# Output projections of a two-layer decoder step by seven products per pair of chunks, with ring slots as scratch

## What is computed

```python
def short_conv_mixer(x, buf, w_in, conv_w, w_out):
    ...
    y = jnp.einsum('bsc,cd->bsd', gb * conv, w_out)
def rglru_mixer(...):
    ...
    y = jnp.einsum('bsc,cd->bsd', jax.nn.gelu(gate, approximate=True) * h, w_out)
def reference(...):
    for i in range(DEPTH):
        yp, nbp = short_conv_mixer(...)
        xp = layer_norm(ALPHA * xp + yp, ln1_g[i], ln1_b[i])
        mp = hier_moe(xp, ...)
        xp = layer_norm(ALPHA * xp + mp, ln2_g[i], ln2_b[i])
```

## Time and profile before

| | us |
|---|---|
| median of 3 runs | 1436.39 (1434.8 to 1436.47) |
| the profiled execution, its own time | 1436.33 |
| its span, first to last instruction | 1434.6 |
| PE busy | 1364.6 (95%) |
| DVE / ACT / POOL busy | 478.9 / 222.3 / 137.5 |
| read from HBM | 468.77 MB |

### The profile page before, as it was taken

The page is one execution under the profiler, slowest core; times in us unless marked ns, Lnnn a source line. Parts: engine busy times, 40 slices in busy tenths (PEclk is TensorE's granted clock), DMA queues, the critical chain, the costliest instruction groups (busy, mean ns, idle before and its releaser), DMA issues.

```text
span 1434.6 us, 20217 instructions
## 1 busy us (share of the span) xinstructions
PE 1364.6 (95%) x8784; PEld 917.3 (64%) x8784; DVE 478.9 (33%) x1016; ACT 222.3 (15%) x372; POOL 137.5 (10%) x143
## 2 busy tenths in 40 slices
PE   7999999899999999999899999989999999999996
PEld 6888876565555555666468887756655555566661
DVE  5666513412111112132255665163111111113316
ACT  1000002100000000100054554030000000110012
POOL 0000000100010001121000000011100110012201
PEclk9999999999999999999999999999999999999999
DMA  9950273899999999999997113279999999999995
GB/s 263 302 231 0 90 322 108 324 426 425 424 425 423 423 426 423 422 427 422 378 324 322 59 60 120 71 279 417 421 426 425 422 426 424 423 425 424 421 403 209
DMA packets 98543, 472.88 MB, mean 330 GB/s; under 512 B 16607, under 2 KB 51423, under 8 KB 63629
## 3 DMA queue, kind: packets, MB, share of 16 engines
q1 hardware_dynamic: 82509, 449.74, 77.6%
q0 software_dynamic: 11520, 15.52, 3.1%
q10 hardware_dynamic: 4424, 6.30, 1.6%
HBM read 468.77 MB, written 27.32 MB: 346 GB/s over the span
## 4 chain that ended last, share of the span: by engine, by line
PE 66%; DMA 7%; DVE 3%; issue 3%; ACT 3%; POOL 0%; POOLq 0%; DVEq 0%
PE ps L970 26%; PE ps L1006 14%; PE ps L650 8%; PE ps L937 6%; DMA ring<-in_moe_w_down 6%; PE ps L750 3%; PE ps L926 3%; PE ps L948 1%; PE ps L768 1%; DMA yrows<-A,Bt 1%; PE ps L994 1%; ACT A L1316 1%; PE ps L986 1%; DMA ring<-yrows 1%; DVE C L1862 1%
## 5 line engine op out<-in xcount | busy, mean ns | idle before, releaser
L970 PE MATMUL ps<-ring,A 128*64 128x256 f32 x4096 | 455.4, 379 | 7.0 <-ACT A L1292 2.4
L970 PEld LDWEIGHTS ps<-ring,A 128*64 128x64 f32 x4096 | 327.5, 137 | 144.8 <-issue 35.1
L1006 PE MATMUL ps<-ring,A 128*64 128x512 f32 x1024 | 233.8, 597 | 24.9 <-issue 22.0
L1781 DVE TENSOR_TENSOR A<-A,ps 128x256 f32<-128x256 f32 x64 | 27.0, 421 | 558.4 <-ACT A L1304 558.4
L1006 PEld LDWEIGHTS ps<-ring,A 128*64 128x64 f32 x1024 | 76.1, 136 | 137.1 <-issue 130.3
L650 PE MATMUL ps<-A,ring 128*128 128x260 f32 x576 | 130.5, 388 | 2.5 <-DMA ring<-in_a_w_in 2.5
L650 PEld LDWEIGHTS ps<-A,ring 128*128 128x128 f32 x576 | 111.0, 193 | 20.2 <-issue 2.7
L750 PE MATMUL ps<-Bt,ring 128*128 128x260 f32 x512 | 116.1, 385 | 1.0 <-ACT C L1210 0.8
L750 PEld LDWEIGHTS ps<-Bt,ring 128*128 128x128 f32 x512 | 96.1, 190 | 20.1 <-DVE A L1588 2.5
L591 POOL DMA_INDIRECT A<-x,idx x42 | 43.6, 1038 | 656.5 <-PE ps L926 605.6
L937 PE MATMUL ps<-C,Bt 104*64 104x512 f32 x400 | 95.5, 619 | 0.0
(11 more groups left out here) (270 smaller groups left out, 1106.4 us busy)
## 6 DMA issues: line engine op xcount, KB each, us to landing
ring<-in_moe_w_gate SPq DMA_DIRECT2D x62, 2048.0 KB, 20.6
ring<-in_moe_w_up SPq DMA_DIRECT2D x60, 2048.0 KB, 22.4
ring<-in_moe_w_down SPq DMA_DIRECT2D x60, 2048.0 KB, 23.5
ring<-in_a_w_in SPq DMA_DIRECT2D x24, 512.0 KB, 7.2
ring<-yrows SPq DMA_DIRECT2D x10, 1024.0 KB, 9.3
ring<-in_moe_w_up SPq DMA_DIRECT2D x8, 1024.0 KB, 21.7
ring<-in_moe_w_down SPq DMA_DIRECT2D x8, 1024.0 KB, 21.4
ring<-in_b_w_in SPq DMA_DIRECT2D x8, 1024.0 KB, 12.6
```

Source lines behind the costliest of these rows:

```text
L970: mm = pe.matmul(ps[hf * ROWS:(hf + 1) * ROWS, 3, u * FH:(u + 1) * FH], xgT[:, k, :], ring[:, slot, col:col + FH], start=(k == 0), stop=(k ...
L1006: mm = pe.matmul(ps[nh * ROWS:(nh + 1) * ROWS, 2, :], hidT[:, at:at + ROWS], ring[:, slot, m * D + nh * 512:m * D + (nh + 1) * 512], start ...
L1781: tt(gated, gated, ps[:, 3, FH:2 * FH], ALU.mult).then_inc(ready, 1)
```

## The change

Each pair of output chunks (2q, 2q+1) is computed by seven products of 4 matmuls (`out_product`), for the blocks a11, a12 (chunk 2q, features 0 to 511 and 512 to 1023) and a21, a22 (chunk 2q+1). POOL forms the sums S1 to S4 of the weights (`out_sums`: 4 + 12 operations on 128x512 in each layer), DVE the pieces T1 to T4 of `hT` (`out_pieces`, on 128x260). The eight products that need only the first four chunks of `hT` (`EARLY`) come first and are copied to SBUF by ACT; the other twenty (`LATE`) are taken out of PSUM by DVE with adds on 128x260. Products rotate over six PSUM banks, each waiting for its bank to be empty (`bank_free`).

Pieces, sums and copies lie in three ring slots of input weights (`SCRATCH`: slots 0, 1, 2 in layer 0, slots 6, 7, 8 in layer 1), which no expert unit may enter until the projection is over. The first ten expert units are therefore spread over the slots in another order (`CYCLE`), and SP waits for them by `room_count`. In layer 0, five units wait for the first early product, the sixth for product (2, 6), and four for `logits(7)`. In layer 1, one unit goes with each of the input units 0 to 3 and the gate unit, the sixth with product (2, 6), and four with `logits(7)`. The early load of two units at L711 is gone, and so is that of three units in layer 1. Three semaphores of the recurrence become one (`act_gate`), with the same waits.

```diff
+DENSE = U_IN[0] + U_OUT
+CYCLE = ((3, 4, 5, 6, 7, 8, 0, 1, 2, 9), (0, 1, 2, 9, 3, 4, 6, 7, 5, 8))
+SCRATCH = ((0, 1, 2), (6, 7, 8))
 def ring_slot(pos):
-    return pos % RING
...
+    if pos < DENSE:
+        return pos
+    l = int(pos >= POS_EXP[1])
+    return CYCLE[l][(pos - POS_EXP[l]) % RING]
...
+EARLY = [(q, i) for q in range(KT // 2) for i in (1, 5)]
+LATE = [(q, i) for q in range(KT // 2) for i in (6, 7, 4, 3, 2)]
+NPART = len(EARLY) + len(LATE)
+OUT_BANKS = ((5, 3, 0, 1, 2, 4), (0, 1, 2, 3, 4, 5))
+COMPLETE = (1, 0, 3, 2, 5, 4, 7, 6)
...
+def room_count(pos):
+    for l in range(DEPTH):
+        if POS_EXP[l] <= pos < POS_EXP[l] + RING:
+            i = pos - POS_EXP[l]
+            if l == 0:
+                return 5 if i < 5 else 6 if i == 5 else DENSE
+            return freed_after(POS_IN[1] + min(i, U_IN[1] + 1))
+    return freed_after(pos - RING)
...
-                    sp.wait_ge(freed, freed_after(pos - RING))
+                    sp.wait_ge(freed, room_count(pos))
...
+            def out_sums(l):
+                pool.wait_ge(mm_in[l], (PLAIN + 14, 1)[l])
+                for q in range(KT // 2):
+                    if q % 2 == 0:
+                        pos = POS_OUT[l] + q // 2
+                        pool.wait_ge(loaded[ring_slot(pos)], load_target(pos))
+                    a21, a22 = out_part_w(l, 2 * q + 1, 0), out_part_w(l, 2 * q + 1, 1)
+                    pool.tensor_tensor(a21, a21, a22, ALU.add).then_inc(sum_ok, 1)
+                for q in range(KT // 2):
+                    pool.wait_ge(sum_ok, KT * l + (KT // 2 if q == 0 else KT // 2 + q))
+                    if q >= 2:
+                        pool.wait_ge(out_mm, NPART * l + len(EARLY) + 5 * (q - 2) + 4)
+                    a11, a12 = out_part_w(l, 2 * q, 0), out_part_w(l, 2 * q, 1)
+                    s1, a22 = out_part_w(l, 2 * q + 1, 0), out_part_w(l, 2 * q + 1, 1)
+                    s2, s3, s4 = (out_sum(l, q, n_) for n_ in range(3))
+                    step(pool.tensor_tensor(s2, s1, a11, ALU.subtract))
+                    pool.tensor_tensor(s3, a22, s2, ALU.subtract)
+                    pool.tensor_tensor(s4, a12, s2, ALU.subtract).then_inc(sum_ok, 1)
...
-                    if u == 2 and i == 0 and k == 0:
-                        mm.then_inc(freed, 2)
...
+            def out_factors(l, q, i):
+                a11, a12 = out_part_w(l, 2 * q, 0), out_part_w(l, 2 * q, 1)
+                s1, a22 = out_part_w(l, 2 * q + 1, 0), out_part_w(l, 2 * q + 1, 1)
+                w = {1: a11, 2: a12, 3: out_sum(l, q, 2), 4: a22, 5: s1, 6: out_sum(l, q, 0), 7: out_sum(l, q, 1)}[i]
+                x = {1: hT[:, :KH, :HALF], 2: hT[:, KH:, :HALF], 3: hT[:, KH:, HALF:]}
+                t = {5: 0, 6: 1, 7: 2, 4: 3}
+                return w, (lambda k: x[i][:, k, :]) if i in x else (lambda k: out_piece(l, t[i], k))
...
-                def logits(m, free=0):
-                    pe.wait_ge(zT_done, KT * l + m + 1)
-                    if m == 0:
+                def logits(n, free=0):
+                    m = COMPLETE[n]
+                    pe.wait_ge(zT_done, KT * l + n + 1)
+                    if n == 0:
                         pe.wait_ge(wg_ok, l + 1)
                     for hf in range(2):
                         mm = pe.matmul(ps[:NC + 2, 6 + hf, :HALF], wr[:, m, :], xT[:, m, hf * HALF:(hf + 1) * HALF],
-                                       start=(m == 0), stop=False)
+                                       start=(n == 0), stop=False)
                         if free and hf == 0:
                             mm.then_inc(freed, free)
...
+                def early_part(n):
+                    q, i = EARLY[n]
+                    if n in (0, 4):
+                        pos = POS_OUT[l] + n // 4
+                        pe.wait_ge(loaded[ring_slot(pos)], load_target(pos))
+                    bank_free(n)
+                    if i == 5:
+                        pe.wait_ge(piece_ok, 5 * l + 1)
+                        pe.wait_ge(sum_ok, KT * l + q + 1)
+                    out_product(l, q, i, n, free=(5 if (l, n) == (0, 0) else 1 if (l, n) == (1, 4) else 0)
+                                ).then_inc(out_mm, 1)
+                pe.wait_ge(h_done[l], KH)
+                for n in range(4):
+                    early_part(n)
                 if l == 1:
-                    pe.wait_ge(ev_a[1], KT)
-                pe.wait_ge(loaded[ring_slot(POS_OUT[l])], load_target(POS_OUT[l]))
-                out_part(l, 0, 0, EARLY, free=(6, 0)[l])
-                if l == 1:
-                    pe.wait_ge(ev_b[1], KT)
-                    out_part(l, 1, 0, EARLY)
                     rg_gates(KT - 1)
-                    pe.wait_ge(sig_ok, 2 * KT)
-                    out_part(l, 2, 0, EARLY, free=1)
-                    pe.wait_ge(h_done[1], KT - 1)
-                    for m in range(3):
-                        out_part(l, m, EARLY, KT - 1)
-                pe.wait_ge(h_done[l], KT)
-                for m in range(KT):
-                    if m == 3:
+                for n in range(4, len(EARLY)):
+                    early_part(n)
+                pe.wait_ge(sum_ok, KT * l + KT // 2 + 1)
+                pe.wait_ge(h_done[l], KT - 1)
+                pe.wait_ge(piece_ok, 5 * l + 2)
+                for n in range(4):
+                    bank_free(late_at(n))
+                    out_product(l, *LATE[n], late_at(n), 0, KH - 1)
+                for n in range(4):
+                    if n < 3:
+                        pe.wait_ge(piece_ok, 5 * l + 3 + n)
+                    else:
+                        pe.wait_ge(h_done[l], KT)
+                    out_product(l, *LATE[n], late_at(n), KH - 1, KH).then_inc(out_mm, 1)
+                for n in range(4, len(LATE)):
+                    q, i = LATE[n]
+                    if late_at(n) == STATE_AT + 2:
+                        bank_free(STATE_AT)
+                        bank_free(STATE_AT + 1)
                         state_rows()
-                    if m in (3, 4, 6, 7):
-                        pe.wait_ge(zT_done, KT * l + {3: 2, 4: 3, 6: 4, 7: 5}[m])
-                    if m == 5:
-                        pe.wait_ge(st_sb, l + 1)
-                    done = ((EARLY, 0, 0), (KT - 1, KT - 1, KT - 1))[l]
-                    if m == FT:
-                        pe.wait_ge(loaded[ring_slot(POS_OUT[l] + 1)], load_target(POS_OUT[l] + 1))
-                    out_part(l, m, done[m] if m < 3 else 0, KT, free=int(m == FT)).then_inc(out_mm, 1)
-                    if m >= 1:
-                        logits(m - 1, free=(1 if m == KT - 1 else 0))
-                logits(KT - 1)
+                    bank_free(late_at(n))
+                    if i == 6:
+                        pe.wait_ge(sum_ok, KT * l + KT // 2 + q + 1)
+                    out_product(l, q, i, late_at(n), free=int((q, i) == (2, 6))).then_inc(out_mm, 1)
+                    if q and i in (6, 7):
+                        logits(2 * q - 2 + (i == 7))
+                logits(KT - 2)
+                logits(KT - 1, free=(4, 1)[l])
...
+                def early_copies(lo, hi):
+                    for n_ in range(lo, hi):
+                        act.wait_ge(out_mm, NPART * l + n_ + 1)
+                        act.activation(out_copy(l, n_), ps[:, out_bank(l, n_), :HALF], ACT.Copy).then_inc(ev_a[l], 1)
+                if l == 0:
+                    early_copies(0, len(EARLY))
...
+                    early_copies(0, 4)
                     recurrence_gates(KT - 1)
+                    early_copies(4, len(EARLY))
...
+            def out_pieces(l, c):
+                k = c % KH
+                t1, t2, t3, t4 = (out_piece(l, t, k) for t in range(4))
+                low, high = hT[:, c, :HALF], hT[:, c, HALF:]
+                dve.wait_ge(h_done[l], c + 1)
+                if c < KH:
+                    ins = tt(t1, high, low, ALU.subtract)
+                    if c == KH - 1:
+                        ins.then_inc(piece_ok, 1)
+                        dve.wait_ge(piece_ok, 5 * l + 1)
+                elif c < KT - 1:
+                    step(tt(t2, high, t1, ALU.subtract))
+                    tt(t3, high, hT[:, k, HALF:], ALU.subtract)
+                    ins = tt(t4, low, t2, ALU.subtract)
+                    if c == KT - 2:
+                        ins.then_inc(piece_ok, 1)
+                else:
+                    tt(t2, high, t1, ALU.subtract).then_inc(piece_ok, 1)
+                    tt(t3, high, hT[:, k, HALF:], ALU.subtract).then_inc(piece_ok, 1)
+                    dve.wait_ge(piece_ok, 5 * l + 3)
+                    tt(t4, low, t2, ALU.subtract).then_inc(piece_ok, 1)
...
+                if j == 0:
+                    for n_ in range(2):
+                        out_pieces(0, c + n_)
...
+                def taken_part(q, j, dst, x):
+                    dve.wait_ge(out_mm, NPART * l + len(EARLY) + 5 * q + j + 1)
+                    tt(dst, x, out_bank_of(q, j), ALU.add).then_inc(ev_b[l], 1)
```

(59 more changed lines are left out.)

109 lines of the change are left out of this document (72 added, 37 removed).

## The result

The changed kernel takes 1448.97 us in the median of 4 executions (1444.88 to 1453.0), the kernel before 1436.43 beside it: ratio 1.0088, 95% interval 1.0067 to 1.0108. The change makes the kernel slower by 0.9%; the forecast was 1430.4 us. The profiled execution took 1453.0 us (span 1451.2, 16.6 us more than the span before).

What follows compares the result with a forecast made beforehand. PE and, slightly slower in expert phases, the DMA weight stream were taken to bound the kernel. Projection savings of 7.0 and 6.1 us less stream lags of 2.7 and 4.4 gave -6.0 us: 1430.4 us, range 1426 to 1433.5.

Steps and rivals of the forecast that it cites:

- -7.0 us: Layer 0's output projection: 16 fewer matmuls on PE shorten it by 7.0 us.
- 57.2 us: Layer 0's output projection: its expected length on PE, in place of 64.2 us.
- rival 2: Input stage of layer 0: DVE falls behind while POOL adds, 4.2 us short, total 1434.6 us; chance 0.08.
- they have 60 us and hide: Layer 0 up to 170 us: POOL's first ten sums have 60 us after the output weights land, costing nothing.
- at nothing: Both layers: DVE's piece subtractions and ACT's eight copies cost no time, covered by DVE's idle time.
- -6.1 us: Layer 1's output projection: ends at 923.1 in place of 929.2, including a PE wait of 3.3 us.
- What the ring slots cost: Behind each projection: four loads released late and three more units make the stream lag 2.7 and 4.4 us.
- PE itself does not wait for these units: After each projection: the four late units cause no PE wait, since the first is expert 2's gate.
- 10.3 us free: Layer 0, 234 to 277 us: DMA room for added loads, by busy share; by bytes 16.0 us.
- as slow as before: Behind the projections: stores of token rows run below 425 GB/s and will take the DMA engines as before.
- Rival 3: PE's wait before products (2, 6) and (3, 6), both layers: late sums, 1450 us; chance 0.12, shared with anything else slower.
- The sum: Whole kernel: -7.0 + 2.7 - 6.1 + 4.4 = -6.0 us, from 1436.33 to 1430.4 us.

Runs made afterwards that it cites:

- The hold alone: The kernel before, with only the loads of units 6 to 8 of each layer's experts issued together with unit 9: ratio 1.0123, 1454.4 us.

## Why the prediction was wrong

- **"-7.0 us" and "57.2 us" in layer 0:** right, 57.3 us. It came to -1.5 in the profiled execution, since rival 2 ate it before the projection began.
- **Rival 2, given 0.08:** right in place and mechanism, wrong in chance and size. The Trainium skill's page on SBUF named a contention of the two engines and no row spoke against it, and still it got a small chance. I priced DVE's loss at 4.2 us but left out the clock behind the pause. Stall and clock are 5.5 us of layer 0 when they occur. What failed in the working is "they have 60 us and hide", said of the first sums on POOL: they start at 87.84 us, beside DVE's own additions, and so the work that was cost "at nothing" did not stay under DVE's idle time.
- **Layer 1, "-6.1 us":** the wait was right, 3.3 us; the clock behind it was missing, 0 to 3 us. In a profile where it did not fall, the projection takes 62.65 us, 5.6 less than before. (The rows' own times put the end of the sigmoid at 873.22, not at the summed 873.0, which is 0.2 us.)
- **"What the ring slots cost", 7.1 us:** the step that decides. The hold alone costs 17.7 us. Two sentences of it failed. "PE itself does not wait for these units" is true of the units and wrong for PE: it waits for rows gathered from x1, whose stores share the DMA engines with them. And the room of "10.3 us free" (by share) to "16.0 us" (by bytes) was taken as if all of it could be used, while the stores, which must run in it, were said to be "as slow as before": in the changed kernel the last one took 18.02 us, and POOL's two 9.8 and 13.0 instead of 5.5 and 6.6. With slots given back early and the stores let through, the same three more units cost 3.3 + 4.0 = 7.3 us in the two stretches of that profile (630.5 and 509.4 against 627.2 and 505.4), near the forecast, though with some of the loads up to 5 us earlier. So the count of the bytes may have been about right, which no run tests by itself; what was missing was the coupling from stores to gather to PE to slots to stream.
- **Rival 3, late sums:** wrong, the sums took 1.36 to 1.60 us in the mean and PE never waited for one. The slower side was given to this mechanism and came by another.
- **The sum:** with the hold at 17.7 us in place of 7.1, up to 5.5 for the stall and up to 3 for the clock, -13.1 becomes +4.6 to +13.1; measured +12.5.

Left open: why a store of token rows, issued beside 20 us of queued loads, lands only with the last of them; whether unit 9 behind the stores would be enough with late slots; and how the clock chooses which pauses it answers.

## What to carry to other kernels

When a change delays loads, follow what else uses the same DMA engines in that stretch, stores above all, to the engine that waits for it and to the buffers which that engine frees; a stream that feeds on freed buffers can lose more to such a loop than to its bytes. If undoing one suspected bound brings nothing, look at what has become late instead and undo both before you drop it: here early slots, worth 0.1% at most alone, and a hold like one that had brought 0.1 to 0.2% gave about 1% together. Put GpSimd's tensor work where VectorE reads PSUM, not where it adds SBUF tiles.

## What the runs showed of the hardware

- Beside a GpSimd sum that reads SBUF, VectorE's addition of two SBUF tiles of 128x512 takes 1.64 us instead of 0.69 and the sum 1.60 to 1.73 instead of 1.27; also a `tensor_scalar` (0.48 to 1.56 us) and a copy of ten columns (0.17 to 1.25 us) are held up. Additions with one input in PSUM (0.45 us) are not.
- Behind one and the same pause of TensorE of 3.3 us, seven profiles show 0.1, 1.5, 1.7, 1.8, 1.8, 3.0 and 3.0 us of loss at the lower clock (1.2 instead of 2.4 GHz). With the pauses for gathered rows the granted clock was 0.50 in each 2 us from 270 to 278 us in the changed kernel (pause of 7.85 us, to 272.34), from 270 to 280 in the kernel before with the slots held (7.23 us, to 272.84), and from 262 to 274 with slots given back early (7.01 us, to 265.81).
- Stores of token rows, from queues of their own, are held up by 2 MB loads of another: the last store took 18.0 us beside four of them, and 8.5 us where two were held back (issued at 245.90, and the held load went out behind its landing at 254.41).
